# Regrouping half-array matmuls by row half, with finer semaphores in the window attention

## The chip, the core and the metric

The kernel runs on one core of a Trainium2 chip. The metric is the device time of one execution in microseconds (us): 3237.68 us, the median of three runs that went from 3231.82 to 3249.09. The engines are TensorE (PE, with its weight loads as PEld), VectorE (DVE), ScalarE (ACT), GpSimd (POOL) and the DMA queues issued by SyncE (SP) and ACT. They run side by side and wait for each other through semaphores, written S("name") in the code.

## The reference

Two transformer blocks are computed in a row over 1024 tokens of width 1024, all in float32. What matters here is the first block's mixing layer, of two parts side by side:

```python
# window attention: 8 query heads over 2 key-value heads, blocks of 128 queries on 256 keys
scores = einsum('bnqhgd,bnkhd->bnhgqk', q, kb) * (HEAD_DIM ** -0.5) + bias   # masked
m = maximum(scores.max(-1), sink);  p = exp(scores - m)
probs = p / (p.sum(-1) + exp(sink - m));  out = einsum('bnhgqk,bnkhd->bnqhgd', probs, vb)

# RWKV-7 recurrence: 8 heads of 64, one step per token
sa = einsum('bhvk,bhk->bhv', state, -kk_t)
state = state * w_t + sa[..., None] * (kk_t * a_t) + v_t[..., None] * k_t
o_t = einsum('bhvk,bhk->bhv', state, r_t)
```

Around them stand the input and output projections, a gated feed-forward layer with a short convolution, and a second block (gated linear attention and stick-breaking attention). These are the same before and after.

## The kernel before

Every engine has one instruction stream, written out by hand; there is no scheduler. Activations lie transposed, with channels on the 128 partitions. The large projections are 161 weight tiles, each multiplied by 1024 tokens in three passes (high and low halves of the float32 values); line 370 issues them. The stages follow each other: norms and first projection, window attention (about 318 to 465 us of the trace), preparation, the chunked RWKV recurrence (about 520 to 925 us), output projection, feed-forward, second block.

A float32 matmul is two records of the trace on PE and two on PEld. Many matmuls of the two stages use half or a quarter of the array. Heads lie in pairs on the partitions: `q` (or `64 * g`) is the slice 0 to 63 for one head of a pair and 64 to 127 for the other. A matmul that reads partitions 0 to 63 uses the upper row half, one that writes PSUM partitions 0 to 63 the first column half. In the trace, `64*64` behind the names is rows times columns in use.

**Window attention.** Eight blocks of 128 queries. In `attend(b, ...)` PE first computes the scores of the next block (line 432, 8 matmuls, `g` is the key-value head and the row half), then transposes the probabilities of this block (line 447) and multiplies them by the values (line 457, two key blocks `kb` by two `g`, where `g` is the column half of the output). Before, one semaphore count stood for both `g`: `att_mm` once per block after the scores, `av_mm` once per block after the products with the values. ACT per block: stage the next block's q, k, v; exponentials; copy both transposes (pT); wait for `av_mm` and copy the outputs of each `g` (proj). `take` waits, and touches one column of a tile called small. DVE per block: scale and bias (sc), maximum, reciprocal and product with the sums' inverse.

**RWKV.** 16 chunks of 64 tokens, two per turn (`s` = 0, 1) in a loop of eight turns. `H2` lists the eight heads as (m, q), for each m both row halves. Per chunk PE makes the group that ends in `ch_mm` (lines 532 to 543, 48 matmuls: products of a chunk with itself, and transposes by the identity), then for five levels `y_mm` (line 554) and `x_mm` (lines 561, 564), then `rhs_mm` (573, 575), `u_mm` (581), `ds_mm` (588, 591) and `o_mm` (598 to 602). All are 64x64 pieces on the diagonal: head half 0 uses rows and columns 0 to 63, the other 64 to 127. DVE and ACT take each group over after one semaphore count.

In one place outside the change, the second block's gated attention, matmuls of alternating column halves are already written two and two (lines 738 to 745; `kh[:, q]` is the stationary tile, so that `q` is the column half):

```python
for h in range(4):
    q = slice(64 * (h % 2), 64 * (h % 2) + 64)
    mm(ps[q, 7, (h // 2) * P:(h // 2 + 1) * P], kh[:, h // 2, q], v_b[:, s, h, :],
       start=True, stop=True)
    i_ = mm(ps[q, 7, 256 + (h // 2) * 64:256 + (h // 2) * 64 + 64], kh[:, 2 + h // 2, q],
            v_b[:, s, 4 + h // 2, q], start=True, stop=True)
```

Of the kernel before, what the change touches and what calls it, by code (L numbers as in the profile page):

```python
# [14 lines left out]
P = 128  # L15
# [71 lines left out]
def build(nc, dr, stop=99):  # L87
    with ExitStack() as ctx:
# [262 lines left out]
        def _(pe):  # L351
# [73 lines left out]
            def scores(b, s, first=False):  # L425
                kb0 = 1 if first else 0
                pe.wait_ge(S("att_stage"), b + 1)
                if not first:
                    pe.wait_ge(S("att_sc"), 2 * b)
                for m in range(4):  # L430
                    for g in range(2):
                        last = mm(ps[:, 2 * g + m // 2, (m % 2) * 256 + kb0 * P:(m % 2) * 256 + 256],
                                  q_st[64 * g:64 * g + 64, s, m, :], k_st[64 * g:64 * g + 64, s, kb0 * P:],
                                  start=True, stop=True)
                last.then_inc(S("att_mm"), 1)

            def attend(b, s, first=False, second=False, last_one=False):
# [12 lines left out]
                pe.wait_ge(S("attT_cp"), 2 * b + 2)  # L450
                if first:
                    pe.wait_ge(S("ada_done"), 1)
                elif not second:
                    pe.wait_ge(S("att_out"), 2 * b - 2)
                for kb in range(kb0, 2):
                    for g in range(2):
                        last = mm(ps[64 * g:64 * g + 64, 6 + s, :], v_st[:, s, kb, 64 * g:64 * g + 64],
                                  pT[:, g, kb, :], start=(kb == kb0), stop=(kb == 1))
                last.then_inc(S("av_mm"), 1)
# [58 lines left out]
            with pe.Fori(0, 8) as i:  # L518
# [6 lines left out]
                for s in range(2):  # L525
# [3 lines left out]
                    for m in range(4):  # L529
                        pairs = [q for mm_, q in H2 if mm_ == m]  # L530
                        for q in pairs:
                            mm(ps[q, z + 0, m * P:(m + 1) * P], b_ch[q, s, m, :], ar[q, s, m, :, :], start=True, stop=True)
                        for q in pairs:
                            mm(ps[q, z + 1, m * P:(m + 1) * P], k_ch[q, s, m, :], ar[q, s, m, :, :], start=True, stop=True)
                        for q in pairs:
                            mm(ps[q, z + 2, m * 64:m * 64 + 64], ar[q, s, m, 0, :], b_ch[q, s, m, :], start=True, stop=True)
                        for q in pairs:
                            mm(ps[q, z + 2, 256 + m * 64:256 + m * 64 + 64], b_ch[q, s, m, :], par("ident")[q, q],
                               start=True, stop=True)
                        for q in pairs:  # L540
                            mm(ps[q, z + 3, m * 64:m * 64 + 64], v_ch[q, s, m, :], par("ident")[q, q], start=True, stop=True)
                        for q in pairs:
                            last = mm(ps[q, z + 3, 256 + m * 64:256 + m * 64 + 64], k_ch[q, s, m, :], par("ident")[q, q],
                                      start=True, stop=True)
                    last.then_inc(S("ch_mm"), 1)

                for l in range(5):
# [9 lines left out]
                    for s in range(2):  # L557
                        hold(S(f"y_cp{s}"), five[l + 1])
                        if l < 4:
                            for m, q in H2:  # L560
                                mm(ps[q, 4 * s, m * 64:m * 64 + 64], xx[q, s, 1, m, :], y_sb[q, s, m, :],  # L561
                                   start=True, stop=True)
                        for m, q in H2:
# [3 lines left out]
                for s in range(2):  # L567
                    hold(S("st_upd"), two[s + 1])
                    hold(S("ch_tok"), two[s + 1])
                    for m in range(4):  # L570
                        pairs = [q for mm_, q in H2 if mm_ == m]
                        for q in pairs:
                            mm(ps[q, 6, m * 64:m * 64 + 64], ar[q, s, m, 0, :], st[q, s, m, :], start=True, stop=False)
                        for q in pairs:
                            last = mm(ps[q, 6, m * 64:m * 64 + 64], m2[q, s, m, 0:64], vk_tok[q, s, 0, m, :],
                                      start=False, stop=True)
# [8 lines left out]
                    for m in range(4):  # L585
                        pairs = [q for mm_, q in H2 if mm_ == m]
                        for q in pairs:
                            mm(ps[q, 6, m * 64:m * 64 + 64], vk_tok[q, s, 1, m, :], vk_tok[q, s, 0, m, :],
                               start=True, stop=False)
                        for q in pairs:  # L590
                            last = mm(ps[q, 6, m * 64:m * 64 + 64], b_tok[q, s, m, :], u_sb[q, m, :],
                                      start=False, stop=True)
                    last.then_inc(S("ds_mm"), 1)
                    hold(S("o_cp"), two[s + 1])
                    for m in range(4):
                        pairs = [q for mm_, q in H2 if mm_ == m]
                        for q in pairs:
                            mm(ps[q, 7, m * 64:m * 64 + 64], st[q, s, m, :], ar[q, s, m, 1, :], start=True, stop=False)
                        for q in pairs:
                            mm(ps[q, 7, m * 64:m * 64 + 64], u_sb[q, m, :], m1[q, s, m, 64:], start=False, stop=False)  # L600
                        for q in pairs:
                            last = mm(ps[q, 7, m * 64:m * 64 + 64], vk_tok[q, s, 0, m, :], m2[q, s, m, 64:],
                                      start=False, stop=True)
# [244 lines left out]
        def _(eng):  # L848
# [93 lines left out]
            def attend(b, s, first=False, last=False):  # L942
# [15 lines left out]
                for g in range(2):  # L958
                    take(S("av_mm"), b + 1)
# [340 lines left out]
        def _(eng):  # L1300
# [547 lines left out]
```

## Time and profile before

| | |
|---|---|
| runs | 3237.68 us median (3231.82 to 3249.09) |
| profiled execution | 3237.68 us, span in the trace 3235.9 us |
| busy, share of the span | PE 84%, PEld 66%, DVE 38%, POOL 25%, ACT 22% |
| mean granted TensorE clock | 0.874 of full speed (2.4 GHz) |
| window attention, 318 to 465 us | PE busy 79.06, DVE 77.05, ACT 82.07 of 147 us |
| RWKV chunks, 520 to 925 us | PE busy 285.12, DVE 193.26, ACT 79.13 of 405 us |

The busy shares are averages over stages. A busy PE is not PE at its peak, since the ends of matmuls are modelled: the length of a record holds a tail in which the next one has already started, and the distance between starts is what a matmul costs in a stream. PEclk of a window is the clock granted to TensorE, 1.0 for 2.4 GHz and 0.5 for 1.2 GHz.

### The profile page before, as it was taken

What the parts mean: (1) busy time and instruction counts of PE and PEld (TensorE: products, weight loads), DVE (VectorE), ACT (ScalarE), POOL (GpSimd) and SP (SyncE); (2) the same over time, 40 slices, a digit from 0 to 9 for tenths busy, and PEclk for the clock granted to TensorE, in tenths of its full rate; (3) what the DMA queues carried; (4) which work ended last, traced back from release to release, by engine and by line L of the source; (5) the groups of instructions that cost most, each with busy time, mean ns of one, the idle gap of its engine ahead of it and who ended that gap; (6) DMA issues with size and microseconds to landing.
All of it is one profiled execution on the core that took longest, in us unless ns stands there. A gap on an engine that the chain in (4) does not pass through costs nothing.

```text
span 3235.9 us, 45658 instructions
## 1 busy us (share of the span) xinstructions
PE 2706.5 (84%) x17970; PEld 2133.0 (66%) x17970; DVE 1213.7 (38%) x1572; ACT 726.4 (22%) x1050; POOL 796.0 (25%) x448
## 2 busy tenths in 40 slices
PE   2899565677689599999999999993999948879986
PEld 1787334666667278888888888871888836653374
DVE  2634536444442653123213213317000056544343
ACT  2111551121121222012102101203111253225521
POOL 1344000000003133433434343340343333210011
PEclk7999657898889799999999999997999955559988
DMA  5411000000002111111111111121211100000031
GB/s 165 156 40 54 5 1 31 3 3 3 3 28 91 65 39 52 45 51 46 46 51 45 52 45 52 45 72 84 91 52 46 46 20 1 0 3 1 0 124 58
DMA packets 34892, 146.85 MB, mean 45 GB/s; under 512 B 3656, under 2 KB 5832, under 8 KB 33608
## 3 DMA queue, kind: packets, MB, share of 16 engines
q1 hardware_dynamic: 23184, 84.42, 7.9%
q10 hardware_dynamic: 11576, 60.50, 5.1%
q8 instruction: 103, 1.69, 0.2%
q14 instruction: 29, 0.24, 0.0%
HBM read 124.46 MB, written 20.45 MB: 45 GB/s over the span
## 4 chain that ended last, share of the span: by engine, by line
PE 72%; DVE 16%; ACT 6%; issue 3%; DMA 2%; DVEq 1%; ACTq 1%; POOL 0%; POOLq 0%
PE ps L370 53%; PE ps L734 2%; DVE xx L76 2%; ACT ab L76 1%; DVE s_m L76 1%; PE ps L787 1%; PE ps L564 1%; DVE proj L76 1%; DVE x_lo L76 1%; DVE lvl L76 1%; DVE ps L76 1%; DMA bias_table<-bias_row 1%; DVE zz L76 1%; PE ps L554 1%; PE ps L561 1%
## 5 line engine op out<-in xcount | busy, mean ns | idle before, releaser
L302 POOL TENSOR_TENSOR w_hi<-w_raw,small 128x1024 fp32r<-128x1024 f32 x161 | 306.5, 1904 | 2200.2 <-PE ps L370 2193.4
L370 PE MATMUL ps<-x_hi,w_hi 128*128 128x512 f32 x2064 | 644.0, 393 | 92.3 <-DVE x_lo L76 85.8
L370 PE MATMUL ps<-x_lo,w_hi 128*128 128x512 f32 x2064 | 639.5, 391 | 0.0
L370 PE MATMUL ps<-x_hi,w_lo 128*128 128x512 f32 x2064 | 639.0, 391 | 0.0
L370 PEld LDWEIGHTS ps<-x_hi,w_hi 128*128 128x128 f32 x2064 | 387.3, 189 | 184.8 <-issue 71.4
L370 PEld LDWEIGHTS ps<-x_lo,w_hi 128*128 128x128 f32 x2064 | 390.2, 189 | 81.7
L370 PEld LDWEIGHTS ps<-x_hi,w_lo 128*128 128x128 f32 x2064 | 389.8, 189 | 81.8
L305 POOL TENSOR_TENSOR w_lo<-w_raw,w_hi 128x1024 fp32r<-128x1024 f32 x161 | 405.8, 2521 | 12.6
L76 DVE SCALAR_TENSOR_TENSOR cv<-ps,cst,cv 128x1023 f32<-128x1023 f32 x64 | 82.1, 1283 | 258.1 <-ACT cv L76 252.7
L370 PE MATMUL ps<-f_hi,w_lo 128*128 128x512 f32 x512 | 157.6, 389 | 0.0
L370 PE MATMUL ps<-f_lo,w_hi 128*128 128x512 f32 x512 | 157.6, 389 | 0.0
L370 PE MATMUL ps<-f_hi,w_hi 128*128 128x512 f32 x512 | 157.6, 389 | 0.0
L76 DVE TENSOR_TENSOR f_acc<-f_acc,ps 128x1024 f32 x32 | 39.1, 1222 | 280.7 <-PE ps L370 280.7
L76 DVE SCALAR_TENSOR_TENSOR cg<-ps,cst,cg 128x1023 f32<-128x1023 f32 x64 | 82.1, 1282 | 152.0 <-ACT cg L76 146.0
L734 PE MATMUL ps<-zz 64*128 64x64 f32 (+2 forms) x896 | 104.1, 403 | 33.8 <-DVE zz L76 33.7
L76 ACT ACTIVATE cg<-ps,cst 128x1024 f32<-128x1024 f32 x32 | 38.7, 1210 | 389.1 <-PE ps L370 389.1
L734 PEld LDWEIGHTS ps<-zz 64*128 64x128 f32 (+2 forms) x896 | 94.3, 304 | 44.3 <-issue 21.8
L387 PE MATMUL ps<-pairs,cst 128*128 128x512 f32 x96 | 63.4, 807 | 70.2 <-DVE pairs L76 70.2
L554 PE MATMUL ps<-xx,lvl 64*64 64x64 f32 x1280 | 60.5, 238 | 63.9 <-DVE lvl L76 49.5
L370 PEld LDWEIGHTS ps<-f_hi,w_lo 128*128 128x128 f32 x512 | 96.1, 188 | 20.0
L370 PEld LDWEIGHTS ps<-f_hi,w_hi 128*128 128x128 f32 x512 | 96.1, 188 | 19.9
L370 PEld LDWEIGHTS ps<-f_lo,w_hi 128*128 128x128 f32 x512 | 96.1, 188 | 19.9
(255 smaller groups left out, 3404.9 us busy)
## 6 DMA issues: line engine op xcount, KB each, us to landing
w_raw<-wall SPq DMA_DIRECT2D x161, 512.0 KB, 3.4
ada_w<-wada ACTq DMA_DIRECT2D x24, 512.0 KB, 5.3
x_spill<-x ACTq DMA_DIRECT2D x2, 4096.0 KB, 11.0
x<-x_spill ACTq DMA_DIRECT2D x2, 4096.0 KB, 13.3
x_in<-xT ACTq DMA_DIRECT2D x2, 2048.0 KB, 12.1
x<-xT ACTq DMA_DIRECT2D x1, 4096.0 KB, 13.5
gate_spill<-gate_st ACTq DMA_DIRECT2D x8, 512.0 KB, 2.6
gate_in<-gate_spill ACTq DMA_DIRECT2D x8, 512.0 KB, 3.3
```

Source lines behind the costliest of these rows:

```text
L76: return emit(*args, **kw)
L302: nc.gpsimd.tensor_tensor(w_hi[:, u, :, :], w_raw[:, u, :, :], sm["one"].unsqueeze(2).to_broadcast([P, KT, P]), ALU.mult).then_inc(S("w_hi ...
L305: nc.gpsimd.tensor_tensor(w_lo[:, u, :, :], w_raw[:, u, :, :], w_hi[:, u, :, :].bitcast(F32), ALU.subtract).then_inc(S("w_split"), 1)
L370: last = mm(ps[:, 2 * u + h, :], w[:, u, k, :], x[:, k, h * 512:(h + 1) * 512], start=(k == 0 and w is w_hi and x is hi), stop=(k == KT - ...
L387: last = mm(rs_of(n)[:, h * 512:(h + 1) * 512], par("mean_all").to_broadcast([P, P]), pairs_of[n][:, j % 2, h * 512:(h + 1) * 512], start= ...
L554: last = mm(ps[q, 4 * s, m * 64:m * 64 + 64], lvl[q, s, l, m, :], xx[q, s, 0, m, :], start=True, stop=True)
L561: mm(ps[q, 4 * s, m * 64:m * 64 + 64], xx[q, s, 1, m, :], y_sb[q, s, m, :], start=True, stop=True)
L564: last = mm(ps[q, 4 * s, 256 + m * 64:256 + m * 64 + 64], y_sb[q, s, m, :], xx[q, s, 1, m, :], start=True, stop=True)
L734: i_ = mm(ps[0:r, 2 * (l % 2) + h % 2, (h // 2) * n:(h // 2 + 1) * n], lh, rh, start=True, stop=True)
L787: last = mm(ps[:, 2 * (n % 2) + x, c:], proj2[q, 11 + h // 2, b * P:(b + 1) * P], proj2[q, 9 + h // 2, t], start=True, stop=True, skip_gro ...
```

## The change

Two things change, both in the order of PE's instructions. In the window attention the loop over `g` becomes the outer one, in the scores and in the products with the values, and each `g` gets its own waits and its own semaphore count. DVE and ACT wait for the count of their `g`. In the RWKV loop, all matmuls of one head in a group are issued one after another, then those of the next head. The number, shapes, operands and destinations of the matmuls stay.

```diff
             def scores(b, s, first=False):
                 kb0 = 1 if first else 0
                 pe.wait_ge(S("att_stage"), b + 1)
-                if not first:
-                    pe.wait_ge(S("att_sc"), 2 * b)
-                for m in range(4):
-                    for g in range(2):
+                for g in range(2):
+                    if not first:
+                        pe.wait_ge(S("att_sc"), 2 * b + g - 1)
+                    for m in range(4):
                         last = mm(ps[:, 2 * g + m // 2, (m % 2) * 256 + kb0 * P:(m % 2) * 256 + 256],
                                   q_st[64 * g:64 * g + 64, s, m, :], k_st[64 * g:64 * g + 64, s, kb0 * P:],
                                   start=True, stop=True)
-                last.then_inc(S("att_mm"), 1)
+                    last.then_inc(S("att_mm"), 1)
...
-                pe.wait_ge(S("attT_cp"), 2 * b + 2)
-                if first:
-                    pe.wait_ge(S("ada_done"), 1)
-                elif not second:
-                    pe.wait_ge(S("att_out"), 2 * b - 2)
-                for kb in range(kb0, 2):
-                    for g in range(2):
+                for g in range(2):
+                    pe.wait_ge(S("attT_cp"), 2 * b + g + 1)
+                    if first and g == 0:
+                        pe.wait_ge(S("ada_done"), 1)
+                    elif not (first or second) and g == 0:
+                        pe.wait_ge(S("att_out"), 2 * b - 2)
+                    for kb in range(kb0, 2):
                         last = mm(ps[64 * g:64 * g + 64, 6 + s, :], v_st[:, s, kb, 64 * g:64 * g + 64],
                                   pT[:, g, kb, :], start=(kb == kb0), stop=(kb == 1))
-                last.then_inc(S("av_mm"), 1)
+                    last.then_inc(S("av_mm"), 1)
...
-                    for m in range(4):
-                        pairs = [q for mm_, q in H2 if mm_ == m]
-                        for q in pairs:
-                            mm(ps[q, z + 0, m * P:(m + 1) * P], b_ch[q, s, m, :], ar[q, s, m, :, :], start=True, stop=True)
-                        for q in pairs:
-                            mm(ps[q, z + 1, m * P:(m + 1) * P], k_ch[q, s, m, :], ar[q, s, m, :, :], start=True, stop=True)
...
+                    for m, q in H2:
+                        mm(ps[q, z + 0, m * P:(m + 1) * P], b_ch[q, s, m, :], ar[q, s, m, :, :], start=True, stop=True)
+                        mm(ps[q, z + 1, m * P:(m + 1) * P], k_ch[q, s, m, :], ar[q, s, m, :, :], start=True, stop=True)
...
-                        if l < 4:
-                            for m, q in H2:
+                        for m, q in H2:
+                            if l < 4:
                                 mm(ps[q, 4 * s, m * 64:m * 64 + 64], xx[q, s, 1, m, :], y_sb[q, s, m, :],
                                    start=True, stop=True)
-                        for m, q in H2:
                             last = mm(ps[q, 4 * s, 256 + m * 64:256 + m * 64 + 64], y_sb[q, s, m, :],
                                       xx[q, s, 1, m, :], start=True, stop=True)
...
-                    take(S("av_mm"), b + 1)
+                    take(S("av_mm"), 2 * b + g + 1)
...
-                    dve.wait_ge(S("att_mm"), b + 1)
+                    dve.wait_ge(S("att_mm"), 2 * b + g + 1)
```

`rhs_mm`, `ds_mm` and `o_mm` are regrouped in the same way: two, two and three matmuls of one head in a row instead of one.

On PE, in the loop over attention blocks: the end of one block (447 the transposes, 457 the products with the values) and the scores of the next (432). An x counts equal instructions.

```order
 L447 MATMUL ps<-cst,sc 128x128 x7
-L454 REGISTER_ALU [waits attT_cp]
+L455 REGISTER_ALU [waits attT_cp]
 L457 MATMUL ps<-pT,v_st 64x512 [waits att_out]
-L457 MATMUL ps<-pT,v_st 64x512 x3
+L457 MATMUL ps<-pT,v_st 64x512
+L457 MATMUL ps<-pT,v_st 64x512 [waits attT_cp]
+L457 MATMUL ps<-pT,v_st 64x512
 L427 REGISTER_ALU
```

The first two products with the values no longer wait for both copies of pT, and stand behind the same transposes as before.

On PE, in the chunk loop, the group that ends in `ch_mm`, before (x2 is one matmul in each of the two halves):

```order
L532 MATMUL ps<-ar,b_ch 64x128 x2
L534 MATMUL ps<-ar,k_ch 64x128 x2
L536 MATMUL ps<-b_ch,ar 64x64 x2
L538 MATMUL ps<-cst,b_ch 64x64 x2
L541 MATMUL ps<-cst,v_ch 64x64 x2
L543 MATMUL ps<-cst,k_ch 64x64 x2
```

and now (rows of head half 0, then of head half 1; line numbers of the changed file):

```order
L530 MATMUL ps<-ar,b_ch 64x128
L531 MATMUL ps<-ar,k_ch 64x128
L532 MATMUL ps<-b_ch,ar 64x64
L533 MATMUL ps<-cst,b_ch 64x64
L535 MATMUL ps<-cst,v_ch 64x64
L536 MATMUL ps<-cst,k_ch 64x64
L530 MATMUL ps<-ar,b_ch 64x128
L531 MATMUL ps<-ar,k_ch 64x128
L532 MATMUL ps<-b_ch,ar 64x64
L533 MATMUL ps<-cst,b_ch 64x64
L535 MATMUL ps<-cst,v_ch 64x64
L536 MATMUL ps<-cst,k_ch 64x64
```

Six matmuls of one head half now stand in a row (with their weight loads and their two records each, 24 instructions), where the halves alternated at every matmul.

## Rows read from the trace of the kernel before

**Rows 1.** The page's chain that ended last, by engine.

```profile
PE 72%; DVE 16%; ACT 6%; issue 3%; DMA 2%; DVEq 1%; ACTq 1%; POOL 0%; POOLq 0%
```

**Rows 2.** Busy time by window; columns: PE, PEld, DVE, ACT, POOL, PEclk, DMA, GB/s.

```profile
318.00:465.00 147.00, 79.06 (x308) 44.76 (x308) 77.05 (x149) 82.07 (x218) 3.71 (x2) 0.63 0.02 8
520.00:925.00 405.00, 285.12 (x7177) 270.68 (x7177) 193.26 (x391) 79.13 (x182) 0.00 (x0) 0.87 0.03 9
```

**Rows 3.** Timeline of one attention block: start, length, engine, line, operation [idle before].

```profile
375.44 3.79 PE L432 MATMUL ps<-k_st,q_st 64*128 64x256 f32 x16 [4.05 <-ACT v_st L76]
...
380.15 1.09 PE L447 MATMUL ps<-cst,sc 128*128 128x128 f32 x8 [0.92 <-DVE sc L76]
...
383.19 1.97 PE L447 MATMUL ps<-cst,sc 128*128 128x128 f32 x8 [1.95 <-DVE sc L76]
383.70 1.46 DVE L76 SCALAR_TENSOR_TENSOR sc<-ps,bias 128x512 f32<-128x512 f32 x2 [0.57 <-issue]
385.19 1.02 ACT L76 ACTIVATE pT<-ps 128x1024 f32<-128x1024 f32 x1 [2.71 <-PE ps L447]
...
386.35 3.68 PE L457 MATMUL ps<-pT,v_st 128*64 128x512 f32 x8 [1.19 <-ACT pT L76]
...
390.07 0.20 ACT L76 ACTIVATE small<-small 128x1 f32<-128x1 f32 x1 [3.85 <-PE ps L457]
390.34 0.59 ACT L76 ACTIVATE proj<-ps 64x512 f32 x1
...
391.36 0.59 ACT L76 ACTIVATE proj<-ps 64x512 f32 x1
...
394.24 3.79 PE L432 MATMUL ps<-k_st,q_st 64*128 64x256 f32 x16 [4.21 <-ACT v_st L76]
```

**Rows 4.** Waits in the attention stage: who for whom, us in total, times, longest.

```profile
ACT small L76 <- PE ps L457: 27.5, 8, 3.9
```

**Rows 5.** Timeline of the chunk stage, iteration at 626.67 us.

```profile
626.67 0.69 PE L532 MATMUL ps<-ar,b_ch 64*64 64x128 f32 x4 [3.79 <-issue]
...
632.96 0.40 PE L532 MATMUL ps<-ar,b_ch 64*64 64x128 f32 x4
...
633.18 0.69 DVE L76 TENSOR_TENSOR m<-ps,rmask 128x512 f32<-128x512 f32 x1 [5.37 <-PE ps L543]
...
636.46 0.30 PE L543 MATMUL ps<-cst,k_ch 64*64 64x64 f32 x4
...
639.80 0.69 DVE L76 TENSOR_TENSOR m<-ps,rmask 128x512 f32<-128x512 f32 x1
```

**Rows 6.** Timeline of the same iteration, two groups of the solver.

```profile
653.92 0.66 PE L561 MATMUL ps<-y_sb,xx 64*64 64x64 f32 x16
...
654.39 0.66 PE L564 MATMUL ps<-xx,y_sb 64*64 64x64 f32 x16
```

**Rows 7.** Timeline of the gated-attention stage: column-half matmuls written two and two.

```profile
2640.49 0.70 PE L742 MATMUL ps<-v_b,kh 128*64 128x128 f32 x4
...
2640.97 0.43 PE L744 MATMUL ps<-v_b,kh 128*64 128x64 f32 x4
...
2641.18 0.69 PE L742 MATMUL ps<-v_b,kh 128*64 128x128 f32 x4
```

**Rows 8.** Timeline of the last attention: four records in one row half.

```profile
2971.45 1.98 PE L787 MATMUL ps<-proj 64*128 64x512 f32 x4 [0.20 <-ACT wts L76]
```

**Rows 9.** Granted clock in the stretches of rows 3, 5, 7 and 8.

```profile
386.35:390.00 3.65, 3.65 (x8) 0.78 (x8) 3.03 (x7) 0.00 (x0) 0.00 (x0) 0.51 0.00 0
626.67:632.30 5.63, 5.63 (x78) 5.63 (x80) 0.85 (x2) 0.00 (x0) 0.00 (x0) 0.50 0.01 3
632.30:636.70 4.40, 4.40 (x118) 4.32 (x114) 3.07 (x7) 0.60 (x1) 0.00 (x0) 1.00 0.02 4
2640.40:2642.00 1.60, 1.60 (x18) 1.41 (x16) 1.32 (x4) 1.18 (x2) 1.60 (x3) 0.50 0.00 0
2971.50:2973.40 1.90, 1.90 (x5) 0.66 (x5) 1.50 (x5) 0.00 (x0) 0.00 (x0) 1.00 0.00 0
```

More of the change, by code:

```diff
@@ L528, in _ @@
                     z = 4 * s
-                    for m in range(4):
-                        pairs = [q for mm_, q in H2 if mm_ == m]
-                        for q in pairs:
-                            mm(ps[q, z + 0, m * P:(m + 1) * P], b_ch[q, s, m, :], ar[q, s, m, :, :], start=True, stop=True)
-                        for q in pairs:
-                            mm(ps[q, z + 1, m * P:(m + 1) * P], k_ch[q, s, m, :], ar[q, s, m, :, :], start=True, stop=True)
[L535 to L544, printed above, removed]
+                    for m, q in H2:
+                        mm(ps[q, z + 0, m * P:(m + 1) * P], b_ch[q, s, m, :], ar[q, s, m, :, :], start=True, stop=True)
+                        mm(ps[q, z + 1, m * P:(m + 1) * P], k_ch[q, s, m, :], ar[q, s, m, :, :], start=True, stop=True)
+                        mm(ps[q, z + 2, m * 64:m * 64 + 64], ar[q, s, m, 0, :], b_ch[q, s, m, :], start=True, stop=True)
+                        mm(ps[q, z + 2, 256 + m * 64:256 + m * 64 + 64], b_ch[q, s, m, :], par("ident")[q, q],
+                           start=True, stop=True)
+                        mm(ps[q, z + 3, m * 64:m * 64 + 64], v_ch[q, s, m, :], par("ident")[q, q], start=True, stop=True)
+                        last = mm(ps[q, z + 3, 256 + m * 64:256 + m * 64 + 64], k_ch[q, s, m, :], par("ident")[q, q],
+                                  start=True, stop=True)
                     last.then_inc(S("ch_mm"), 1)
@@ L569, in _ @@
                     hold(S("ch_tok"), two[s + 1])
[L570 to L576, printed above, removed]
+                    for m, q in H2:
+                        o = ps[q, 6, m * 64:m * 64 + 64]
+                        mm(o, ar[q, s, m, 0, :], st[q, s, m, :], start=True, stop=False)
+                        last = mm(o, m2[q, s, m, 0:64], vk_tok[q, s, 0, m, :], start=False, stop=True)
                     last.then_inc(S("rhs_mm"), 1)
@@ L584, in _ @@
                     hold(S("u_cp"), two[s + 1])
[L585 to L592, printed above, removed]
+                    for m, q in H2:
+                        o = ps[q, 6, m * 64:m * 64 + 64]
+                        mm(o, vk_tok[q, s, 1, m, :], vk_tok[q, s, 0, m, :], start=True, stop=False)
+                        last = mm(o, b_tok[q, s, m, :], u_sb[q, m, :], start=False, stop=True)
                     last.then_inc(S("ds_mm"), 1)
                     hold(S("o_cp"), two[s + 1])
[L595 to L603, printed above, removed]
+                    for m, q in H2:
+                        o = ps[q, 7, m * 64:m * 64 + 64]
+                        mm(o, st[q, s, m, :], ar[q, s, m, 1, :], start=True, stop=False)
+                        mm(o, u_sb[q, m, :], m1[q, s, m, 64:], start=False, stop=False)
+                        last = mm(o, vk_tok[q, s, 0, m, :], m2[q, s, m, 64:], start=False, stop=True)
                     last.then_inc(S("o_mm"), 1)
```

## The prediction

> **What bounds the kernel now.** I read the chain of waits first: PE holds 72% of it [rows 1], so in most stages a PE instruction is late only if it costs PE time or comes late itself. Then the busy time of the two stages that are touched [rows 2]: in attention PE, DVE and ACT are each busy for 77 to 82 of 147 us, so none of them is the bound and the stage is a loop of waits; in the chunk stage PE is busy for 285 of 405 us. Last the timelines, to see which wait ends last.
>
> *Attention* [rows 3]. One block takes 394.24 - 375.44 = 18.80 us. PE computes the next scores at 375.44, transposes at 380.15 and 383.19, idles 1.19 us until ACT has copied the second transpose (385.19 to 386.21), and multiplies by the values from 386.35 to 390.03. ACT waited 3.85 us for that, then does for each g a touch and a copy (390.07 to 390.93 and 391.01 to 391.95), stages the next block and so releases the next scores (4.21 us idle on PE before them). So copy of pT, products with the values, ACT's two output copies and staging are in one ring. The scores are not late: they end at 379.23, and DVE takes them at 383.70.
>
> *Chunks* [rows 5]. One turn of the loop is about 50 us, eight turns are 400 of the 405 us. The first ch_mm group runs from 626.67 to about 632.96 + 0.2, and DVE, idle for 5.37 us, starts on it at 633.18: on the path. The second group runs from 632.96 to about 636.6, and DVE takes it at 639.80: 3 us of slack. Behind that the solver's groups alternate with short copies on ACT and additions on DVE, so nearly all of them are on the path.
>
> **What order means on PE.** Does PE run the two halves at once, and must they alternate for it? The first: four records of 512 columns in one row half took 1.98 us at full clock [rows 8, 9], so about 0.43 each with a tail of 0.27. The products with the values were eight such records at half clock (0.51), 0.86 each, thus 6.8 us one by one; they took 3.68 [rows 3, 9]. Two column halves ran at once. The solver: 16 records of 64 columns start within 654.39 - 653.92 = 0.47 us, 0.029 each [rows 6]; by 512 columns for 0.43, one alone would be 0.053. Also two at once.
>
> The second is what the change rests on. The gated attention writes its column halves two and two: 742, 744 of half 0, then 742, 744 of half 1. The trace shows four records of 742 in one row from 2640.49, and only then, at 2640.97, four of 744 [rows 7]: the 742 of half 1 started before the 744 of half 0 that stands ahead of it in the program. At half clock [rows 9] the first four matmuls took 2641.18 - 2640.49 = 0.69 us; one by one they would be, by 1.71 us for a matmul of 512 columns at half clock, 2 x (0.43 + 0.21) = 1.28. So PE kept both halves busy although two matmuls of one half (8 instructions with weight loads) stood in a row.
>
> The Trainium skill says otherwise ("TensorE: Matmul & The Clock Gate", Part 3, "The mechanism"): "MATMULs are pc-monotone in start AND end — strict FIFO, no reordering". By that rule the halves overlap only where they meet in the program; it is the case "in order" below. The trace disagrees at the one place that it shows.
>
> **The change part by part.** The profiled execution took 3237.68 us, which is also the median, so the sums are made against 3237.7.
>
> 1. *Products with the values in two parts.* The part of g = 0 no longer waits for the second copy of pT. It stands behind the second transposes, which end at 385.16, so it starts about 1.1 us earlier and, at 3.68 us, is done at about 388.9. ACT's touch and copy for g = 0 (0.94 us from touch to touch, 390.07 to 391.01) then lie beside the rest of g = 1. The part of g = 1 starts at 386.35 as before, beside the second matmul of g = 0, and ends at 390.03; then come one touch and one copy instead of two. Gain 0.94 to 1.0 us a block, and ACT waits there 8 times [rows 4]: -8 us. What is late next is still g = 1; exponentials of the next block wait for DVE's maxima, some 2 us earlier. Behind the new wait of g = 1 on PE stand only its own two matmuls and the next scores, which wait for ACT anyway. Bounds: if the two parts don't overlap at all, g = 1 ends at 388.9 + 3.5 = 392.4 instead of 390.03, and after one ACT copy less the loss is 1.4 us a block, +11 us; the other end is -8, and -16 with the clock (below).
>
> 2. *Scores in two parts.* DVE takes them 4.5 us after they end: no gain. If the two halves overlap as before, no loss. One by one they would take at most 3.79 us more at half clock; PE has 0.92 us idle before 380.15 and 1.95 before 383.19, so most is covered: 0 to +1 us a block. I take 0. The extra wait is satisfied when it is reached (DVE took the earlier scores a block ago).
>
> 3. *ch_mm, runs of six.* The work is the same. If PE starts the other half over 24 instructions, the cost is only a later start of half 1 after a wait. I take 0.1 us a turn. One by one and in order: a warm group costs 636.57 - 632.96 = 3.6 us with both halves busy, 7.2 without; seven borders save 0.11 each: 6.4. The first group has half clock for 5.63 us [rows 9], worth 2.8 warm; the remaining 3.6 make it 9.2 instead of 6.3, +2.9 us a turn. The second grows by 2.8 and DVE, itself 2.9 later, takes it in time. If the reach is just the two matmuls of rows 7, each border saves 0.23: 5.6 for a warm group, and 5.63 + 2.8 = 8.4 for the first: +2.1 us a turn. So 0 to +23 us; a gain has no source, since both halves are busy already.
>
> 4. *x_mm, rhs_mm, ds_mm (two in a row), o_mm (three).* Two in a row is the pattern of rows 7: no cost. In order, each group of 16 matmuls takes nine slots instead of eight, each slot 0.117 warm (0.47 / 4) or twice that: about 7 x_mm groups on the path, two of them at half clock, make +1.0 a turn; rhs and ds 4 x 0.117 = +0.5; o has 24 matmuls, 17 slots instead of 12, once on the path (the other lies before the 3.79 us in which PE is idle at the head of the loop [rows 5]), +0.6. Together 0 to +2.1 us a turn, +17. For three in a row, one past what rows 7 show, I take 0.
>
> Sum: -8 + 0 + 8 x 0.1 + 0 = -7: 3237.7 - 7 = 3230.7, I say 3231.
>
> **Rivals.**
> - *Short reach.* PE starts past two matmuls but not past six. For it: rows 7 show no more than two. Against: nothing in the trace; it just isn't tested. 3237.7 - 8 + 8 x 2.1 = 3246.5. It becomes a loss from a price of 1 us a turn.
> - *In order.* The halves overlap only at borders. Slower: ch_mm +2.9, the rest +2.1 a turn, 8 x 5.0 = +40; attention gains about 5 (g = 1 starts half a microsecond late). 3237.7 + 40 - 5 = 3273. Rows 7 speak against it, unless what two column halves do is not done by the diagonal quarters, or not at full clock: rows 7 are at half clock and in column halves only.
> - *The split doesn't pay.* The products of g = 1 queue behind those of g = 0 although the halves differ, because the wait stands between them: +11 in attention, 3249; with a partial overlap about 3240. Against: at its arrival the first matmul of g = 0 is nearly through.
> - *The clock.* In attention it averaged 0.63 [rows 2], and the products ran at 0.51 [rows 9] after 1.19 us of idle PE. Without the gap PE is busy from 383.19 to 390. If the clock rises within that stretch, up to half of the last 2 us is saved, 1 us a block: 3223. The 1.97 and 3.68 us before, with their small gap, were not enough; and it could as well shift the other way somewhere.
>
> **How the numbers follow.** Forecast as worked out (3226 to 3236) 0.57; short reach 0.13; in order 0.13; split that doesn't pay 0.09; clock 0.08. The measurement can tell about 0.5% (16 us) from no change: faster is below 3221.5, slower above 3253.9. Faster: half of the clock case and a tail of the first, 0.09. Slower: in order, a quarter of the short reach (if other groups suffer too) and a little of the split, 0.19. Same: 0.72. Range for 8 in 10: from 3221 (clock) to 3254, which takes in short reach and split and leaves in order and a part of the clock case out. The likeliest case's own range is 3226 to 3236.
>
> **What would show it.** In the changed profile the block period of attention should be about 17.8 us instead of 18.80; ACT's first touch after the products should start near 388.9 on the old scale, some 1.1 us before the second; PE's idle time before the products with the values should be nearly gone for g = 0. The ch_mm groups should run from start to start in 6.3 and 3.6 us, and an x_mm group in 0.47 at full clock; records of the two halves should interleave in time although the program has six of one in a row. If ch_mm takes 8.4 or more, the reach is short; if o_mm and x_mm also grow, by 5/12 and 1/8, it is in order. PE's busy time in the chunk stage, 285 us, should stay; a rise by more than 10 us would prove me wrong there, and a block period of 18.8 or more in attention.

## The result, and the profile after

The changed kernel takes 3294.47 us (median of four runs, 3289.98 to 3300.53), the kernel before 3241.61 (four runs, 3231.82 to 3249.09): a ratio of 1.0162, with a 95% interval of 1.0138 to 1.0185. It is slower by 53 us where 7 us less was forecast. The profiled executions have spans of 3291.8 and 3235.9 us, so 55.9 us are to be found.

The page's chain of the changed kernel, by engine; PE has four points more than in [rows 1]:

```profile
PE 76%; DVE 14%; ACT 5%; issue 3%; DMA 2%; DVEq 1%; ACTq 0%; POOL 0%; POOLq 0%
```

Windows of the changed kernel, with the columns of [rows 2]: both stages (the second starts earlier and ends later now, from 513.73 to 974.7 us, and its window takes that in), then one turn of the chunk loop in five pieces, then one block's products with the values in two.

```profile
318.00:465.00 147.00, 99.93 (x348) 65.79 (x348) 79.05 (x151) 89.54 (x224) 3.58 (x2) 0.66 0.02 8
512.00:975.00 463.00, 375.91 (x7168) 364.52 (x7168) 188.16 (x384) 70.53 (x172) 0.00 (x0) 0.75 0.01 2
630.90:632.00 1.10, 1.08 (x16) 1.10 (x17) 0.84 (x2) 0.00 (x0) 0.00 (x0) 1.00 0.05 15
632.00:641.50 9.50, 9.50 (x88) 9.50 (x86) 0.19 (x2) 0.17 (x1) 0.00 (x0) 0.50 0.01 2
641.50:651.90 10.40, 10.40 (x100) 10.40 (x100) 5.46 (x12) 0.42 (x1) 0.00 (x0) 0.50 0.01 2
652.00:659.30 7.30, 4.28 (x78) 4.12 (x75) 3.77 (x8) 1.36 (x3) 0.00 (x0) 0.50 0.00 0
659.30:688.00 28.70, 21.23 (x630) 19.92 (x626) 12.87 (x26) 7.10 (x18) 0.00 (x0) 1.00 0.01 3
383.93:385.90 1.97, 1.97 (x5) 1.01 (x6) 1.69 (x4) 1.02 (x1) 0.00 (x0) 0.50 0.00 0
385.90:387.60 1.70, 1.69 (x6) 0.39 (x3) 1.39 (x3) 0.50 (x2) 0.00 (x0) 0.90 0.00 0
```

The chunk stage has the same 7168 records (the window of [rows 2] holds nine more, from behind the stage), yet PE is busy for 376 us where it was 285, and the granted clock fell from 0.87 to 0.75. The pieces of the turn show where: both ch_mm groups run in a stretch at half clock, nearly from their start to their end. Before, the first ran at half clock for 5.63 us and then at full, and the second at full [rows 9]. The stretch at half clock in which the solver begins was there before as well, in the same turn of the kernel before:

```profile
642.50:649.40 6.90, 5.74 (x103) 5.62 (x105) 2.64 (x5) 0.72 (x2) 0.00 (x0) 0.51 0.00 0
```

The timeline of the same turn, changed kernel; L530 to L536 are the six products of one head half:

```profile
630.92 0.40 PE L530 MATMUL ps<-ar,b_ch 64*64 64x128 f32 x2 [3.71 <-issue]
...
631.50 0.28 PE L533 MATMUL ps<-cst,b_ch 64*64 64x64 f32 x2
631.61 0.22 PE L535 MATMUL ps<-cst,v_ch 64*64 64x64 f32 x1
631.62 0.32 PE L530 MATMUL ps<-ar,b_ch 64*64 64x128 f32 x1
...
632.62 0.31 PE L535 MATMUL ps<-cst,v_ch 64*64 64x64 f32 x1
632.62 0.47 PE L530 MATMUL ps<-ar,b_ch 64*64 64x128 f32 x1
...
633.96 0.31 PE L535 MATMUL ps<-cst,v_ch 64*64 64x64 f32 x1
633.96 0.47 PE L530 MATMUL ps<-ar,b_ch 64*64 64x128 f32 x1
...
641.33 0.69 DVE L76 TENSOR_TENSOR m<-ps,rmask 128x512 f32<-128x512 f32 x1 [9.31 <-PE ps L536]
...
652.05 0.69 DVE L76 TENSOR_TENSOR m<-ps,rmask 128x512 f32<-128x512 f32 x1 [4.25 <-PE ps L536]
```

Two things are to be seen. First the reach: the other half's first record (L530) starts with or just behind the first L535 record. At that moment three records of the first half that stand ahead of it in the program have not started: the second L535 and both of L536. So of the twelve starts of a run nine are spent one after another, and three lie beside the other half. Second the price: from run to run it is 633.96 - 632.62 = 1.34 us, eight times a group, 10.7 us. DVE gets the first group 10.41 us after PE starts it (6.51 before, [rows 5]) and the second 10.72 us later (6.62 before): +3.9 and +4.1 in this turn. Over the first seven turns the means are 5.85 us before and 10.92 after for the first, 6.62 and 10.72 for the second, and 36.77 and 36.57 from there to the next turn: +5.1, +4.1 and -0.2. The whole +9.0 a turn lies in the two ch_mm groups, and nothing of it in the solver.

The waits of the two stages in the changed kernel (who for whom, us, times, longest), first attention, then chunks:

```profile
ACT small L76 <- PE ps L457: 14.5, 8, 2.2
...
ACT vk_tok L76 <- PE ps L536: 177.4, 16, 12.6
...
DVE m L76 <- PE ps L536: 111.6, 16, 10.3
```

The first was 27.5 us [rows 4]. The others are the new bound of the chunk stage. The same two before, where DVE waited for ch_mm only once a turn:

```profile
ACT vk_tok L76 <- PE ps L543: 80.2, 16, 7.7
...
DVE m L76 <- PE ps L543: 37.3, 8, 5.4
```

One attention block of the changed kernel, beside [rows 3]:

```profile
382.06 1.94 PE L447 MATMUL ps<-cst,sc 128*128 128x128 f32 x8 [1.21 <-ACT pT L76]
...
383.93 3.66 PE L457 MATMUL ps<-pT,v_st 128*64 128x512 f32 x8
...
384.04 1.02 ACT L76 ACTIVATE pT<-ps 128x1024 f32<-128x1024 f32 x1 [2.12 <-PE ps L447]
...
387.03 0.20 ACT L76 ACTIVATE small<-small 128x1 f32<-128x1 f32 x1 [1.97 <-PE ps L457]
387.30 0.59 ACT L76 ACTIVATE proj<-ps 64x512 f32 x1
387.97 0.20 ACT L76 ACTIVATE small<-small 128x1 f32<-128x1 f32 x1
388.32 0.59 ACT L76 ACTIVATE proj<-ps 64x512 f32 x1
...
391.22 5.65 PE L432 MATMUL ps<-k_st,q_st 64*128 64x256 f32 x16 [3.63 <-ACT v_st L76]
...
396.79 1.97 PE L447 MATMUL ps<-cst,sc 128*128 128x128 f32 x8
```

The products with the values start with no gap, while ACT still copies the second transpose. ACT's second touch (387.97) no longer waits. The scores take 5.65 us where they took 3.79, and the transposes follow with no idle time: here the scores are late.

The 55.9 us by stage, from the starts of records: attention (last projection to the last product with the values) -8.9; preparation of the chunks (to the first ch_mm record) -5.1; chunk stage +70.8; from its end to the output projection -6.4; all the rest, which holds nothing changed, +5.6. In the second and fourth the work is the same, and the time at half clock is less by 11 and 14 us.

### The profile page after: what moved, and what is told of

The parts are those of the page before. It is cut to its first block, busy times and chain, and to the rows that moved or that the text cites. A ratio compares the mean times of both kernels' runs of the same rounds, so it can differ in the third digit from the quotient of the medians.

```text
span 3291.8 us, 45652 instructions
## 1 busy us (share of the span) xinstructions
PE 2815.3 (86%) x17970; PEld 2240.3 (68%) x17970; DVE 1213.9 (37%) x1572; ACT 726.0 (22%) x1050; POOL 795.9 (24%) x448
## 4 chain that ended last, share of the span: by engine, by line
PE 76%; DVE 14%; ACT 5%; issue 3%; DMA 2%; DVEq 1%; ACTq 0%; POOL 0%; POOLq 0%
PE ps L370 52%; PE ps L715 2%; PE ps L531 2%; ACT ab L76 1%; DVE s_m L76 1%; PE ps L768 1%; DVE x_lo L76 1%; DVE proj L76 1%; DVE xx L76 1%; PE ps L556 1%; DVE ps L76 1%; DMA bias_table<-bias_row 1%; PE ps L547 1%; PE ps L530 1%; DVE zz L76 1%
## 5 line engine op out<-in xcount | busy, mean ns | idle before, releaser
L715 PE MATMUL ps<-zz 64*128 64x64 f32 (+2 forms) x896 | 103.8, 403 | 33.7 <-DVE zz L76 33.7
L530 PE MATMUL ps<-ar,b_ch 64*64 64x128 f32 x256 | 85.4, 435 | 41.4 <-issue 26.1
L370 PEld LDWEIGHTS ps<-f_hi,w_lo 128*128 128x128 f32 x512 | 96.1, 188 | 19.9
L370 PEld LDWEIGHTS ps<-f_lo,w_hi 128*128 128x128 f32 x512 | 96.1, 188 | 19.9
```

The source lines that it names most:

```text
L370: last = mm(ps[:, 2 * u + h, :], w[:, u, k, :], x[:, k, h * 512:(h + 1) * 512], start=(k == 0 and w is w_hi and x is hi), stop=(k == KT - ...
L715: i_ = mm(ps[0:r, 2 * (l % 2) + h % 2, (h // 2) * n:(h // 2 + 1) * n], lh, rh, start=True, stop=True)
```

## The experiments

In the table, "turn" is the mean distance of two starts of the chunk loop in the profiled execution (seven distances), "half clock" what of a turn of the chunk stage ran at 1.2 GHz, and "attention" the stage as above. Ratios are to the kernel before on the same chip, where its median was 3237.43 us (e1 to e4), 3237.60 (e5, e7 to e9), 3239.09 (e6, e10 to e12) and, in a single run, 3229.50 (e13, e14).

| kernel | us | ratio (95%) | turn | half clock a turn | attention |
|---|---|---|---|---|---|
| before | 3241.61 | 1 | 49.24 | 12 | 145.2 |
| changed | 3294.47 | 1.0162 (1.0138-1.0185) | 58.21 | 29 | 136.3 |
| e1, attention only | 3226.14 | 0.9965 (0.9946-0.9984) | 49.15 | 12 | 137.2 |
| e5, products with the values only | 3224.10 | 0.9955 (0.9940-0.9970) | 49.22 | 13 | 134.1 |
| e6, scores only | 3245.55 | 1.0013 (0.9994-1.0031) | 49.24 | 12 | 152.2 |
| e3, all but ch_mm | 3231.06 | 0.9981 (0.9967-0.9994) | 49.63 | 13 | 137.4 |
| e12, x, rhs, ds, o only | 3239.68 | 1.0008 (0.9992-1.0023) | 49.61 | 13 | 145.2 |
| e4, ch_mm three in a row | 3243.25 | 1.0016 (1.0000-1.0032) | 50.01 | 12 | 146.4 |
| e7, four in a row | 3251.53 | 1.0046 (1.0032-1.0061) | 51.03 | 14 | 146.2 |
| e2, six in a row (ch_mm only) | 3303.13 | 1.0208 (1.0191-1.0225) | 58.13 | 30 | 145.5 |
| e8, 24 in a row | 3345.11 | one run | 62.98 | 36 | 146.9 |
| e9, six, with full-array matmuls added | 3411.84 | one run | 71.68 | 44 | 145.8 |
| e10, six in the second group only | 3242.05 | 1.0012 (0.9997-1.0028) | 49.09 | 11 | 146.3 |
| e11, six in the first group only | 3278.59 | 1.0129 (1.0103-1.0156) | 54.41 | 20 | 146.9 |
| e13, 24 in the second group only | 3236.20 | one run | 49.68 | 11 | 145.4 |
| e14, e2 with its first group issued twice | 3280.68 | one run | 54.78 | 10 | 147.1 |

The attention stage is one profile of each kernel. In the eleven profiles in which its code is unchanged it takes 145.2 to 147.1 us, with 109 to 127 us of that at half clock.

**Which part costs.** e1 makes only the attention part, e2 only the runs of six in ch_mm, e3 all except these.

> Only the attention half of the change (both loops over g outside, with counts per g); the chunk loop as before. All theories that put the loss into the chunk loop: attention stage about 9 us shorter, as in the changed kernel (first to last start of the products with the values 116.4 us against 124.9), whole kernel 3228 to 3236, ratio about 0.997. If the changed attention shifted the clock of later stages for the worse, the kernel is slower than 3245 and the turns of the chunk loop are longer than 49.2 us.

> Only the ch_mm group in runs of six matmuls of one half; everything else as before. Theory 'short reach and clock': the whole loss is here, 58.4 us a turn of the chunk loop against 49.2, +60 to +75 us on the kernel (3302 to 3316), with the granted clock at 0.5 from about 1 us after the start of the group to its end. Rival 'short reach alone': +2.1 us a turn, +17, 3259. Rival 'the other groups of the chunk loop': within 10 us of before.

> The changed kernel with the ch_mm group put back into alternating halves; attention, x_mm, rhs_mm, ds_mm and o_mm stay regrouped. 'Short reach and clock': all of the loss gone, turns of 49.2 us, the attention gain left, 3228 to 3236, faster than before by 0.2 to 0.5%. Rival 'the other groups cost too': turns of 51 us or more, 3250 or more.

e2's edit, the diff shown ahead of the prediction for ch_mm alone:

```diff
-                    for m in range(4):
-                        pairs = [q for mm_, q in H2 if mm_ == m]
-                        for q in pairs:
-                            mm(ps[q, z + 0, m * P:(m + 1) * P], b_ch[q, s, m, :], ar[q, s, m, :, :], start=True, stop=True)
...
+                    for m, q in H2:
+                        mm(ps[q, z + 0, m * P:(m + 1) * P], b_ch[q, s, m, :], ar[q, s, m, :, :], start=True, stop=True)
...
```

e1 has the attention hunks of that diff, e3 all its hunks but this one. e2 has the whole loss and more: 58.13 us a turn, as in the changed kernel. The attention part gains 8.0 us in its stage.

**How far PE reaches.** e4, e7 and e8 issue the same 48 products with 3, 4 or 24 of one half in a row:

```diff
+                    todo = [[a for m in range(4) for a in products(m, slice(64 * h, 64 * h + 64))] for h in range(2)]
+                    for n in range(0, 24, 3):
+                        for h in range(2):
+                            for a in todo[h][n:n + 3]:
+                                last = mm(*a, start=True, stop=True)
```

> Before, with the ch_mm group in runs of three matmuls of one half. If PE starts a record past three or four unissued ones of the other half, a run of six records still overlaps almost fully, as o_mm does in the changed kernel: a warm group 3.9 us instead of 3.6, clock up after the first 5.6 us, turns of 49.2 to 49.8 us, kernel within 6 us of before. In-order theory (halves overlap only at borders): 5.6 us and more for a warm group, and with the clock lost turns of 55 us or more, 3285 or more.

> Before, with the ch_mm group in runs of four matmuls of one half. By a reach of three unissued records a warm group takes 4.4 us (3.7 when alternating, 5.4 with runs of six). 'Reach and clock': with 85% of the time in two quarters the clock still comes up as before, so the first group grows by about 0.9 us, turns of 50.3 us, kernel +9. If the clock is lost here too, turns of 54 us or more, +40. 'Order alone' (loss proportional to lost overlap, 8.9 us a turn for 1.7 us of a warm group): turns of 52.9 us, +29.

> Before, with all 24 matmuls of one half first and then the 24 of the other: one quarter of the array works alone for nearly the whole group while PE is never idle in it. 'Clock follows how much of the array works': the granted clock stays at 0.5 through both groups, each takes 14.3 us, turns of 65 us. 'Clock follows whether PE is busy': it rises to 1.0 after some 6 us as before, groups of about 10 and 7.2 us, turns of 53 us.

The turn grows by 0.8, 1.8, 8.9 and 13.7 us with 3, 4, 6 and 24 in a row. With a reach of three records the halves lose their overlap gradually: of two products in a row (four records) one would stand alone, of six nine. The step between four and six isn't gradual; it is where the time at half clock jumps from 14 to 30 us a turn. Two windows of e7 (four in a row), at the head of a turn:

```profile
631.00:637.40 6.40, 6.40 (x70) 6.40 (x71) 1.17 (x3) 0.00 (x0) 0.00 (x0) 0.50 0.02 5
637.40:644.00 6.60, 6.24 (x143) 6.10 (x140) 4.52 (x10) 1.23 (x3) 0.00 (x0) 1.00 0.01 2
```

Here the clock comes back inside the groups, as before.

**More work beside the runs.** e9 puts two matmuls of the whole array, by the identity, ahead of each pair of runs of six (16 more records a group; what they write is overwritten at once):

```diff
+                    for m, q in H2:
+                        if q.start == 0:
+                            for _ in range(2):
+                                mm(ps[:, z + 0, m * P:(m + 1) * P], par("ident"), ar[:, s, m, :, :].rearrange("p a c -> p (a c)"), start=True, stop=True)
```

> ch_mm in runs of six, with eight additional full-array matmuls (128x128, 128 columns; the result is overwritten) in each group, two ahead of each m: more work and less overlap. 'Clock follows how much of the array works': it could come up, and then a warm group takes about 9.3 us (6.4 for runs of six that overlap at the border inside each m, 1.7 of added work, some 1.2 for changing the array's division) against 10.7 now at half clock, so the second group is shorter than with runs of six alone. If the clock stays down, 18.6 us a group and turns of 73 us.

33.7 us of a turn of e9, which hold all of its two groups but the first 1.1 us and the last 0.3:

```profile
671.30:705.00 33.70, 33.70 (x224) 31.30 (x225) 5.71 (x13) 0.60 (x1) 0.00 (x0) 0.50 0.00 1
```

PE is busy without a gap by its records, part of it with the whole array, and the clock stays at half throughout. The test is not clean: where the whole array follows a quarter or a quarter the whole array, two starts lie 0.35 to 0.37 us apart instead of 0.21, so e9 adds breaks as well as work.

**Which group, and from which clock.** Up to here I held that the clock falls when one quarter of the array works alone. e10 and e11 make runs of six in only one of the two groups of a turn. The first meets half clock, after the 3.8 us in which PE is idle at the head of the loop; the second meets full clock.

```diff
+                    if s == 1:
+                        for m, q in H2:
+                            mm(ps[q, z + 0, m * P:(m + 1) * P], b_ch[q, s, m, :], ar[q, s, m, :, :], start=True, stop=True)
...
+                    else:
+                        for m in range(4):
...
```

(e11 has `s == 0` there.)

> Before, with runs of six only in the ch_mm group of the second chunk of a turn (s = 1), which in the kernel before runs wholly at full clock and has 3 us of slack before DVE takes it. 'Clock falls when one quarter works alone': the group starts at 1.0 and the clock falls to 0.5 inside it although PE is never idle; the group takes 7 to 10 us instead of 3.6, DVE waits for it, and turns grow by 2 to 5 us, +15 to +40 on the kernel. 'Reach alone': 5.4 us at full clock to the end, hidden in the slack, turns of 49.2 to 49.5, kernel as before.

> Before, with runs of six only in the first group of a turn (s = 0). The group ran at half clock for 5.6 of 6.3 us before. 'Clock': it stays at 0.5 to its end, 10.7 to 11.1 us, +4.5 a turn, and the second group (alternating) starts at 0.5 and brings the clock up within some 6 us: turns of 53 to 55 us, +30 to +45 on the kernel. 'Reach alone': first group 8.2 us, turns of 51.2, +16.

The second group of e10, then the first of e11:

```profile
634.20:640.20 6.00, 6.00 (x109) 6.00 (x106) 5.06 (x11) 0.60 (x1) 0.00 (x0) 1.00 0.01 3
```

```profile
634.20:645.50 11.30, 11.30 (x100) 11.30 (x102) 0.93 (x3) 0.00 (x0) 0.00 (x0) 0.50 0.01 1
```

Equal instructions: at full clock, which holds, the group takes 5.8 us of the first window; at half clock, which also holds, 10.7 of the second. In all eight turns of e10 the second group has full clock throughout; in all eight of e11 the first is at half clock from 1.4 us behind its start at the latest, to its end. My theory of that time fell with e10: the runs don't lower the clock. In e10 the group is 2.2 us longer than before, within the 3 us of slack that [rows 5] show: DVE takes it 6.62 us after the first, as before, and the turn is unchanged. e11's turn grows by 5.2 us, and its clock comes back only in the second group, which alternates.

Left open was whether even longer runs would lower the clock, and whether a clock that has been brought up would survive both groups. e13 is e10 with 24 in a row. e14 is e2 with the first group issued twice over, alternating and then in runs of six (the same values are written again):

```diff
+                    if s == 0:
+                        for m in range(4):
+                            pairs = [q for mm_, q in H2 if mm_ == m]
...
                     for m, q in H2:
                         mm(ps[q, z + 0, m * P:(m + 1) * P], b_ch[q, s, m, :], ar[q, s, m, :, :], start=True, stop=True)
```

> Only the second chunk group of each turn is issued with its 24 products of one partition half in a row, then the 24 of the other; the first group, which meets the clock at half after the idle at the head of the loop, alternates as before. Measured so far: with runs of six in that place the group took 5.8 us at full clock (0.725 us a run) and the turn stayed at 49.1 us. Theory A (the state on arrival: runs of one quarter do not bring the clock up, but do not bring it down either): the group takes 24 products of one quarter, less three records, at full clock, about 7.1 us, the granted clock stays 1.0, the turn is 49 to 50.5 us. Theory B (one quarter alone lowers the clock, only more slowly than six at a time show): the granted clock falls to half inside the group, the group takes 10 us or more, the turn is 53 us or more.

> Both chunk groups in runs of six, as in the experiment that did this alone (turn 58.1 us), but the first group is issued twice: first alternating (as before), which in the kernel before brings the granted clock back to 1.0, and then again in runs of six over the same results. That is 96 more matmul records a turn, about 3.7 us of work at full clock and up to 6.3 us with half of it at half clock. Theory A (the state on arrival decides): after the alternating pass both groups in runs of six run at full clock, 5.8 us each, granted clock 1.0 in them, and the turn is 53 to 56 us, less than 58.1 although there is more to do. Theory B (runs of six lower the clock whatever came before): windows of granted clock 0.5 over both groups of runs, 10.4 us each, and the turn is 62 to 65 us.

e13's second group; then e14's alternating pass up to the rise of the clock, the rest of it with the runs of chunk 0, and the runs of chunk 1:

```profile
634.60:641.80 7.20, 7.20 (x113) 7.20 (x109) 5.64 (x12) 0.60 (x1) 0.00 (x0) 1.00 0.01 2
```

```profile
637.00:640.00 3.00, 2.96 (x40) 2.99 (x42) 0.89 (x3) 0.00 (x0) 0.00 (x0) 0.50 0.02 5
640.10:648.30 8.20, 8.20 (x160) 8.20 (x157) 0.05 (x1) 0.05 (x1) 0.00 (x0) 1.00 0.01 4
648.30:654.00 5.70, 5.70 (x103) 5.70 (x103) 4.94 (x11) 0.55 (x1) 0.00 (x0) 1.00 0.00 0
```

Both came out as theory A said, in every one of their eight turns, though each was run only once. In e13 the slack is used up: DVE takes the second group 7.03 us after the first instead of 6.62, and the turn grows by 0.4. e14 issues 96 records a turn more than e2 and is faster, 54.78 against 58.13 us a turn: the alternating pass brings the clock to full in 3 us, and the runs behind it keep it. What decides here is the clock on arrival, and that such runs don't raise it.

**The parts of the attention.** e5 splits only the products with the values (with ACT's wait), e6 only the scores (with DVE's wait):

```diff
-                pe.wait_ge(S("attT_cp"), 2 * b + 2)
...
+                for g in range(2):
+                    pe.wait_ge(S("attT_cp"), 2 * b + g + 1)
...
-                    take(S("av_mm"), b + 1)
+                    take(S("av_mm"), 2 * b + g + 1)
```

> Only the products with the values in two parts (and ACT's count per g); scores as before. If the gain of the attention is this split, the stage is about 8 us shorter than before (137 us from the last record of the projection to the last product, against 145) and the kernel 3226 to 3232, as with both splits. If the gain came from the scores or from the clock, 3 us or less.

> Only the scores in two parts, products with the values as before. The run of one half is eight records there, so the last four of one half and the first four of the other overlap: a scores group costs up to 1.9 us more at half clock, most of it in PE's idle time before the transposes. Attention stage 145 to 149 us, kernel 3237 to 3243; no gain, since DVE takes the scores 4.5 us after they end. If the count per g brings scores forward to DVE, the stage is shorter than 143 us.

e5's stage is 11.1 us shorter, e6's 7.0 longer (5.1 against the longest unchanged stage of the other profiles); in the kernel's time e6 is not to be told from no change. A block of e6:

```profile
379.44 5.65 PE L432 MATMUL ps<-k_st,q_st 64*128 64x256 f32 x16 [4.05 <-ACT v_st L76]
...
385.01 1.97 PE L447 MATMUL ps<-cst,sc 128*128 128x128 f32 x8
```

The scores of one g are four matmuls in one row half, eight records; at half clock they take 5.65 instead of 3.79 us: thirteen starts some 0.43 us apart and three beside the other half, so the reach is three records in row halves too. The 1.86 us more are over the 0.92 us of idle time that stood ahead of the transposes [rows 3].

**The other groups.** e12 makes two in a row in x_mm, rhs_mm and ds_mm and three in o_mm:

> Before, with only x_mm, rhs_mm, ds_mm and o_mm regrouped (two, two, two and three matmuls of one half in a row). 'Reach of three unissued records': all of them overlap fully, turns of 49.2 to 49.7 us, kernel within 5 us of before. In order: turns of 51.3, +17.

+0.4 us a turn, as in e3 (49.63), and in total within 0.3% of before. e12's edit is the last chunk hunk of the diff and its likes. That two in a row cost x_mm nothing is seen in the changed kernel, where eight records take 665.99 - 665.76 = 0.23 us and so 16 take 0.47, as in [rows 6]:

```profile
665.76 0.33 PE L554 MATMUL ps<-y_sb,xx 64*64 64x64 f32 x4
665.88 0.33 PE L556 MATMUL ps<-xx,y_sb 64*64 64x64 f32 x4
665.99 0.33 PE L554 MATMUL ps<-y_sb,xx 64*64 64x64 f32 x4
```

## Why the prediction was wrong

- **Step 3, "ch_mm, runs of six", failed.** It took 0.1 us a turn, on the reading that rows 7 showed PE starting the other half past what stood ahead. It does, but past three records and no further. Rows 7 could have told this: four records stood in a row there, and a reach of three is all they need. The rival *short reach* named it, at a chance of 0.13.
- **The price of the short reach failed too.** The prediction gave +2.1 us a turn, 3246.5 in all. At full clock the mechanism costs what was said: in e10 a run follows the last by 0.725 us, eight of them 5.8, where 5.6 was worked out. But both that sum and the one for *in order* let the first group have half clock for the same 5.63 us as before, and the second none. The runs don't end the half clock: +8.9 us a turn (e2), of which e11 has 5.2. The other 3.7 are the second group's, which costs nothing when it meets full clock (e10) and nearly doubles in length when it doesn't. Eight turns give 71 us, which is the +70.8 of the chunk stage.
- The clock was among the rivals only for attention, with half a sentence that it could shift the other way somewhere; whether the change could keep it down in the loop was not asked. Rows 9 held the sign: the head of the turn was at half clock, and full clock came back during the very group that was changed. The turn read there is also a long one: 50.01 us, where the mean is 49.24 and eight turns are 390 us, not 400.
- **Step 1, the products with the values, was right.** The forecast was -8; e5 shows -11.1 in its stage. The gap before the products is gone, ACT's first touch comes 3.10 us after the products start, and the second is 0.94 later as worked out. From block to block the products start 16.5 us apart in e5 (mean of six), 18.3 before; 17.8 was forecast. The extra 3 us go with the rival *the clock*: with no gap ahead the granted clock rises within the products (0.90 from 385.90 to 387.60 in the changed kernel, and in every block of e5), and e5 has 17 us less at half clock in the stage than before (92 against 109). That the clock is their cause was not tested.
- **Step 2, the scores, was mis-sized.** "0 to +1 us a block, I take 0" measured +7.0 us in all (e6), 0.9 a block: near the upper bound. The two halves overlap only by three records of eight, and the cover was smaller than the bound on the loss. With step 1 it is -8.0 (e1), which hides the miss: the forecast -8 was right for the sum and for neither part.
- **Step 4, the other groups, was right** within its bounds of 0 to +17: the turn of e12 grows by 0.37 us, 3 us in all.
- PE's busy time in the chunk stage was to stay at 285 us, and a rise by more than 10 us was to prove the prediction wrong there. It rose to 376.

On order, the rule of the Trainium skill ("TensorE: Matmul & The Clock Gate", Part 3, "The mechanism"), "strict FIFO, no reordering", is not what the traces show: L530 starts ahead of three records before it in the program. In effect it was nearer the truth than my reading, since beyond three records the order is kept: strictly in order a warm group was to take 6.4 us, it takes 5.8 (e10), and alternating 3.6.

The same page of the Trainium skill (Part 1, "What's actually happening") says of the clock that "activity releases the throttle". By that a PE that is busy without a gap should come to full clock. Here it was busy for 9.50 of 9.50 us and then 10.40 of 10.40 at half clock, and for 33.70 in e9. The trace disagrees as far as busy time stands for activity.

What stays open: why runs of six at half clock don't bring it back while runs of four and alternating halves do, and why full-array matmuls beside them (e9) didn't help. No run here tells what raises the clock, nor whether runs of one quarter would keep a full clock for longer than the two groups of e14 did. The +5.6 us in the unchanged rest aren't explained; the same stretch varies by 12 us among these kernels (2256.5 to 2268.8), and with it goes its time at half clock: 477 to 489 us in the six kernels where it is shortest, 499 to 533 in the other ten (484 before, 533 in the changed kernel). The -5.1 and -6.4 us in the neighbouring stages go with less time at half clock there, which is a reading and was not tested.

The best version is e5: only the products with the values split, 3224.10 us, 0.9955 of before (0.9940 to 0.9970). Its interval overlaps with e1's, so that it is better than both splits together rests on the stage times (134.1 and 137.2 us).

## What to carry to other kernels

In these traces, matmuls on different halves or quarters of the array overlap only if no more than three records stand between them in the program: alternate them, and keep to one or two float32 matmuls of one half or quarter in a row. Before touching the order of a group on PE, read the granted clock on both sides of it; where the group follows an idle stretch and the clock comes back within it, that return is part of what is changed. Splitting a group so that its first part starts before the last copy pays where the consumer waits and gains nothing where nobody does, so measure the two splits apart.

## What the runs showed of the hardware

- PE starts a matmul of another half or quarter ahead of up to three records that stand before it: in quarters at both clocks (L530 and L535 at 631.62 and 632.62), in row halves at both (scores at 379.44 in e6, at 425.0 in the changed kernel), in column halves at half clock [rows 7].
- One group of 48 quarter matmuls in runs of six takes 5.8 us at full clock and 10.7 at half; alternating 3.6 at full. Runs of six (e14, two groups) and of 24 (e13, one group) did not lower a full clock; runs of six didn't raise a half one in 19.9 us (632.00 to 651.90), nor did runs of 24 in e8, where both groups of every turn ran at half clock to their end.
- PE busy without a gap for 33.7 us, partly with the whole array, stayed at half clock (e9).
- At the head of the loop (turns two to eight), after 3.6 to 3.9 us of idle PE, the granted clock of the changed kernel fell to 0.5 between 2.0 us before and 1.2 us behind the first record (1.1 us behind it in the turn shown). In the kernel before, which alternates, it fell there too, between 1.4 us before and 0.2 behind. So the fall goes with the idle time and not with the runs.
